# A merge stage whose branch products move from f32 matmuls to three-term split matmuls

## The chip, the cores and the metric

The kernel runs on one core of a Trainium2 chip. The metric is the device time of one execution in microseconds (us), the median of several runs. Engine names follow the profile: PE (TensorE, matmul), PEld (its weight load), DVE (VectorE), ACT (ScalarE), POOL (GpSimd), SP (SyncE, which here only sends DMAs).

## The reference

The program is two blocks in a row on a sequence of 1024 tokens of width 1024. The first has two layers, each with two recurrent branches; the second is attention, pooling and a mixture of experts. The change touches only the end of each layer of the first block, here called the merge:

```python
for l in range(DEPTH):                       # DEPTH = 2
    ...
    y_hg = o_hg.astype(x.dtype) @ w_branch_hg[l]       # (1024 x 512) @ (512 x 1024)
    ...
    y_rw = y_rw.astype(x.dtype) @ w_branch_rw[l]       # (1024 x 512) @ (512 x 1024)
    g_hg, g_rw = jnp.split(p_gate, N_BRANCH, axis=-1)
    merged = jax.nn.sigmoid(g_hg) * y_hg + jax.nn.sigmoid(g_rw) * y_rw
    out = merged @ w_out[l]                            # (1024 x 1024) @ (1024 x 1024)
    x = layer_norm(DN_ALPHA * x + (1.0 + gate_raw[:, None]) * out, ln_g[l], ln_b[l])
```

## The kernel before

The program is a chain of stages with a barrier of all engines behind each. `merge(k, l)` runs twice, once for each layer. Everything is held transposed: features on the 128 partitions in 8 tiles (`KT`), tokens along the free axis. The tokens are worked in two halves of 512 (`HALF`, `hf` = 0 and 1). Within a half there are two phases:

- Branch phase, 8 tiles (`branches(m)` on PE, m = 8 hf + j). For output tile j, PE makes the two branch products in f32, four matmuls each, from the raw weights `wb` (two buffers) and the branch outputs that the stages before left in `k.mix` (`k.yhg` and `k.yrw` are its halves). ACT takes the sigmoid of the loaded gates `sg` (`gates`). DVE (`merged`) multiplies both products by their gates (L2170), adds them (L2172), and splits the sum into a rounded high part (L2176, a CAST to float32r) and the rest, the low part (L2178). The two parts of all 8 tiles are `mS`.
- Product phase, 8 tiles (`product(q)` on PE). The weight slab `w` of output tile j is split the same way: ACT rounds it (`high`, L2123), POOL subtracts (L2109). PE then sums three products for each of 8 slices, in the order of `TERMS`: high x high, high x low, low x high, so 24 matmuls in one tile. ACT scales the result (`residual`), DVE adds it to the residual stream `xT` (`add`).

The layer norm over features follows: sums over the partitions by f32 matmuls with ones (`mean`, `variance`), `centre`, `squares`, `deviation` (rstd) and `normalise`. For the first half these are placed by hand in the branch phase of the second half; for the second half they stand at the end of the stage.

The order on each engine is the order of the code. Between the engines there are only semaphores that count finished operations: `hi_ready` and `lo_ready` for the parts of a slab, `slab_done` for a finished product tile, `ys_ready` for a finished branch product (two to a tile), `m_ready` and `mul_done` for DVE's multiplications and add, `low_ready` for the low part of `mS`. Each ring has two buffers: `w` and its parts `wS`, `wb`, `sg`, and the banks of `ps`. The loops of a stage are unrolled.

Of the kernel before, what the change touches and what calls it, by code (L numbers as in the profile page):

```python
# [2050 lines left out]
def merge(k, l):  # L2051
# [4 lines left out]
    with Stage(k, f"mix{l}") as s:  # L2056
        mS = s.sb("mS", [P, 2, KT, HALF], F32R)
        gate, lnp = s.sb("gate", [P, KT]), s.sb("lnp", [P, 2, KT])
        w, wS = s.sb("w", [P, 2, KT, P]), s.sb("wS", [P, 2, 2, KT, P], F32R)
        wb = s.sb("wb", [P, 2, KT, P])  # L2060
# [3 lines left out]
        ld_w, ld_wb, ld_sg = ([s.sem(f"{n}{b}") for b in range(2)] for n in ("ld_w", "ld_wb", "ld_sg"))  # L2064
# [10 lines left out]
        @block.sync
        def _(sp):
            def branch(m):
# [1 line left out]
                wait(sp, ys_ready, 2 * (m - 1))
                sp.dma_start(wb[:, b, 0:4], I["w_branch_hg"][l, j]).then_inc(ld_wb[b], 16)  # L2080
                sp.dma_start(wb[:, b, 4:8], I["w_branch_rw"][l, j]).then_inc(ld_wb[b], 16)
# [7 lines left out]
            sp.dma_start(lnp[:], I["ln_par"][l]).then_inc(ld_p, 16)
            branch(0)  # L2090
            branch(1)
            for hf in range(2):
                for j in range(2 if hf == 0 else 4, NJ):
                    branch(hf * NJ + j)
                    if j == 4 or j == 5:
                        slab(hf * NJ + j - 4)
                for j in range(2, NJ):
                    slab(hf * NJ + j)
                    if hf == 0 and j >= 6:
                        branch(NJ + j - 6)  # L2100
                if hf == 0:
                    branch(NJ + 2)
                    branch(NJ + 3)
# [35 lines left out]

# [1357 lines left out]
```

## Time and profile before

| | |
|---|---|
| median of 3 runs | 4628.94 us (4622.33 to 4638.01) |
| the profiled execution | 4627.36 us |
| its span, first to last instruction | 4625.1 us |
| PE busy | 4062.8 us, 88% of the span |
| DVE, ACT, POOL busy | 1684.2, 1205.4, 719.3 us |
| mean granted PE clock | 0.928 of full speed |
| first merge, first DMA issue to the next stage's first | 1125.76 to 1374.20 us |

The profile counts an engine as busy while one of its instructions runs. Matmuls overlap in PE's pipeline, so the duration of one record is longer than the distance between two; the price of a matmul is read from distances. An f32 matmul leaves two records in the trace, a float32r matmul one. Times in a timeline are microseconds from the start of the span.

### The profile page before, as it was taken

How to read it: one execution, taken by the hardware profiler on the slowest of the kernel's cores; microseconds unless marked ns; L12 is line 12 of the kernel's file. 1: busy time of each engine (PE TensorE's matmuls, PEld its weight loads, DVE VectorE, ACT ScalarE, POOL GpSimd, SP SyncE). 2: the span in 40 equal slices, each digit the busy share in tenths (PEclk: the TensorE clock that was granted, in tenths of full speed). 3: DMA queues.
4: the chain of work that ended last, by engine and by line, in shares of the span. 5: the costliest groups of instructions: out<-in, count | busy, mean ns of one | idle time of the engine just before them, and what ended most of it. 6: DMA issues, size and time to landing. Idle time of an engine off the chain costs nothing. (4 is left out here: it accounts for less than half of the span.)

```text
span 4625.1 us, 74505 instructions
## 1 busy us (share of the span) xinstructions
PE 4062.8 (88%) x29460; PEld 2648.0 (57%) x29460; DVE 1684.2 (36%) x2437; ACT 1205.4 (26%) x1715; POOL 719.3 (16%) x554
## 2 busy tenths in 40 slices
PE   6999888887979998888879978887889999999963
PEld 3888667665547887666655544535544444444423
DVE  3355554553341004545533426522511111111128
ACT  1111354442221112454422334412111111111114
POOL 2222122120122221131111100000010000000014
PEclk8999998898999999998889989997999999999985
DMA  6765333113313423331123217001089999999967
GB/s 218 216 220 177 124 112 123 53 44 117 127 68 134 141 100 121 107 126 63 39 88 123 86 44 295 35 32 58 19 303 356 351 360 359 356 357 355 355 249 263
DMA packets 289081, 795.16 MB, mean 172 GB/s; under 512 B 29377, under 2 KB 121026, under 8 KB 252994
## 3 DMA queue, kind: packets, MB, share of 16 engines
q1 hardware_dynamic: 240738, 616.41, 38.3%
q10 hardware_dynamic: 25632, 93.33, 5.0%
q0 software_dynamic: 22464, 81.80, 4.9%
q8 instruction: 195, 3.19, 0.3%
q14 instruction: 52, 0.43, 0.0%
HBM read 622.64 MB, written 160.43 MB: 169 GB/s over the span
## 5 line engine op out<-in xcount | busy, mean ns | idle before, releaser
L463 PE MATMUL ps<-s_proj_hS,s_proj_wS 128*128 128x512 f32 x3216 | 768.7, 402 | 62.5 <-POOL s_proj_wS L353 62.5
L463 PEld LDWEIGHTS ps<-s_proj_hS,s_proj_wS 128*128 128x128 f32 x3216 | 615.0, 192 | 212.3 <-ACT s_proj_wS L413 63.4
L518 PE MATMUL ps<-gate_h,gate_w 128*128 128x512 f32 x1536 | 417.9, 424 | 33.8 <-PEq L146 19.3
L518 PEld LDWEIGHTS ps<-gate_h,gate_w 128*128 128x128 f32 x1536 | 296.2, 198 | 136.9 <-issue 52.1
L3181 PE MATMUL ps<-s_exp_gu,keep_hT 128*128 128x512 f32 x736 | 340.9, 606 | 19.8 <-DMA s_exp_gu<-in_w_gu_dram 18.0
L3165 PE MATMUL ps<-s_exp_wd,s_exp_aT 128*128 128x512 f32 x736 | 331.2, 593 | 1.9 <-ACT s_exp_aT L3091 1.9
L3186 PE MATMUL ps<-s_exp_gu,keep_hT 128*128 128x512 f32 x736 | 330.8, 592 | 0.0
L505 POOL TENSOR_TENSOR gate_w<-gate_raw,gate_w 128x512 fp32r<-128x512 f32 x128 | 186.4, 1459 | 824.3 <-ACT gate_w L499 823.5
L3131 DVE TENSOR_TENSOR s_exp_sg<-s_exp_sg,ps 128x256 f32<-128x256 f32 x92 | 38.7, 421 | 666.6 <-ACT s_exp_sg L3112 666.6
L353 POOL TENSOR_TENSOR s_proj_wS<-s_proj_w,s_proj_wS 128x1024 fp32r<-128x1024 f32 x67 | 174.0, 2599 | 565.4 <-ACT s_proj_wS L413 565.4
L381 DVE COPY s_proj_o<-ps 128x512 f32<-128x512 f32 x66 | 45.5, 690 | 570.3 <-PE ps L463 570.3
L2225 PE MATMUL ps<-keep_mix,s_mix_wb 128*128 128x512 f32 x512 | 224.6, 600 | 27.1 <-DMA s_mix_wb<-in_w_branch_rw_dram 27.1
L3186 PEld LDWEIGHTS ps<-s_exp_gu,keep_hT 128*128 128x128 f32 x736 | 139.9, 190 | 176.3 <-issue 169.9
L3181 PEld LDWEIGHTS ps<-s_exp_gu,keep_hT 128*128 128x128 f32 x736 | 134.1, 192 | 166.9 <-issue 157.9
L3065 POOL COPY s_exp_idx<-keep_idx 128x1 int32 (+1 forms) x92 | 16.8, 183 | 1286.2 <-PE ps L3148 878.9
L3123 DVE COPY keep_hT<-ps 128x512 f32<-128x512 f32 x184 | 126.5, 687 | 246.3 <-PE ps L3165 223.7
L3165 PEld LDWEIGHTS ps<-s_exp_wd,s_exp_aT 128*128 128x128 f32 x736 | 132.7, 190 | 134.6 <-issue 132.5
L413 ACT ACTIVATE s_proj_wS<-s_proj_w 128x1024 fp32r<-128x1024 f32 x67 | 70.8, 1059 | 496.4 <-DVE s_proj_o L381 228.9
L2237 PE MATMUL ps<-s_mix_mS,s_mix_wS 128*128 128x512 f32 x768 | 193.7, 409 | 2.1 <-DVE s_mix_mS L2178 2.1
L3091 ACT ACTIVATE keep_hT<-ps 128x512 f32<-128x512 f32 x184 | 109.9, 597 | 327.1 <-PE ps L3165 273.6
L2225 PEld LDWEIGHTS ps<-keep_mix,s_mix_wb 128*128 128x128 f32 x512 | 98.4, 193 | 152.9 <-issue 123.6
L2237 PEld LDWEIGHTS ps<-s_mix_mS,s_mix_wS 128*128 128x128 f32 x768 | 144.5, 188 | 47.2 <-issue 11.5
(451 smaller groups left out, 5854.1 us busy)
## 6 DMA issues: line engine op xcount, KB each, us to landing
s_exp_gu<-in_w_gu_dram SPq DMA_DIRECT2D x184, 1024.0 KB, 10.8
s_exp_wd<-in_w_down_dram SPq DMA_DIRECT2D x92, 1024.0 KB, 9.1
yrow<-keep_hT ACTq DMA_DIRECT2D x92, 512.0 KB, 9.5
keep_mix<-in_w_ada_dram SPq DMA_DIRECT2D x80, 512.0 KB, 6.0
s_proj_w<-in_w_in_dram SPq DMA_DIRECT2D x66, 512.0 KB, 4.6
proj<-s_proj_o ACTq DMA_DIRECT2D x66, 512.0 KB, 2.7
gate_raw<-in_w_in_dram SPq DMA_DIRECT2D x128, 256.0 KB, 3.1
yrow<-keep_xT SPq DMA_DIRECT2D x4, 8192.0 KB, 49.1
```

The lines of the kernel that those rows point to most:

```text
L353: pool.tensor_tensor(wS[:, b, 1], w[:, b], wS[:, b, 0], ALU.subtract).then_inc(lo_ready, 1)
L413: act.activation(wS[:, b, 0], w[:, b], ACT.Copy).then_inc(hi_ready, 1)
L463: mm = pe.matmul(k.ps[:, 6 + half if last else 2 * b + half, :], wS[:, b, x, t, :], hS[:, y, t, half * HALF:(half + 1) * HALF], start=(t = ...
L505: pool.tensor_tensor(self.w[:, n % RING, 1], self.raw[:, n % 2], self.w[:, n % RING, 0], ALU.subtract).then_inc(self.split_low, 1)
L518: mm = pe.matmul(self.k.ps[:, self.banks[g // 2], :], weight[:, w, t - t0, :], self.k.hG[:, h, t, :], start=(t == 0 and w + h == 0), stop= ...
L2225: mm = pe.matmul(k.ps[:, 2 * b + g, :], wb[:, b, 4 * g + x, :], y[:, x, cut(hf)], start=(x == 0), stop=(x == 3))
L2237: mm = pe.matmul(k.ps[:, 4 + b, :], wS[:, b, u, x, :], mS[:, v, x, :], start=(x == 0 and u + v == 0), stop=(x == KT - 1 and u == 1))
L3091: return act.activation(o, i, ACT.Copy)
L3123: return dve.tensor_copy(o, i)
L3165: mm = pe.matmul(k.ps[:, 4 + half, :], aT[:, f, :], wd[:, u, f, half * HALF:(half + 1) * HALF], start=(f == 0), stop=(f == 1))
L3181: mm = pe.matmul(k.ps[:, 2 if u == 0 else 6, :], xT[:, u, t, :], gu[:, u, t, :], start=(t == 0), stop=False)
L3186: mm = pe.matmul(k.ps[:, 2 if u == 0 else 6, :], xT[:, u, t, :], gu[:, u, t, :], start=False, stop=(t == KT - 1))
```

## The change

The branch products now work as the output products do, on split parts. `wb` is gone. One ring of slabs, numbered z = `at(hf, j, out)`, carries the branch weights (`out` = 0) and `w_out` (`out` = 1) in the order in which PE takes them, each loaded by two DMAs; ACT and POOL split all 32 of a merge. The branch outputs are split as well, into `yS`: `inputs(0, x)` at the start of the stage, `inputs(1, x)` one slice behind each product tile of half 0. PE's branch tile is 24 matmuls in place of 8. On DVE, `normalise(0)` moves from the branch phase of half 1 into its product phase, one tile behind each `add`.

```diff
+        yS = s.sb("yS", [P, 2, KT, HALF], F32R)
-        wb = s.sb("wb", [P, 2, KT, P])
...
+        def at(hf, j, out):
+            return 2 * NJ * hf + NJ * out + j
+        def used(eng, z):
+            hf, out, j = z // (2 * NJ), z // NJ % 2, z % NJ
+            if out:
+                eng.wait_ge(slab_done, NJ * hf + j + 1)
+            else:
+                eng.wait_ge(ys_ready, 2 * (NJ * hf + j + 1))
...
+            def slab(z):
+                hf, out, j, b = z // (2 * NJ), z // NJ % 2, z % NJ, z % 2
+                wait(sp, lo_ready, z - 1)
+                for x in range(2):
+                    src = I["w_out"][l, j, :, 4 * x:4 * x + 4, :] if out else I[("w_branch_hg", "w_branch_rw")[x]][l, j]
+                    sp.dma_start(w[:, b, 4 * x:4 * x + 4], src).then_inc(ld_w[b], 16)
...
+            for z in range(4 * NJ):
+                pool.wait_ge(hi_ready, z + 1)
+                pool.tensor_tensor(wS[:, z % 2, 1], w[:, z % 2], wS[:, z % 2, 0], ALU.subtract).then_inc(lo_ready, 1)
...
+            def high(z):
+                if z < 4 * NJ:
+                    act.wait_ge(ld_w[z % 2], 32 * (z // 2 + 1))
+                    if z >= 2:
+                        used(act, z - 2)
+                    act.activation(wS[:, z % 2, 0], w[:, z % 2], ACT.Copy).then_inc(hi_ready, 1)
+            def inputs(hf, x):
+                if hf:
+                    act.wait_ge(ys_ready, 2 * NJ)
+                act.activation(yS[:, 0, x], k.mix[:, x, cut(hf)], ACT.Copy).then_inc(yh_ready, 1)
...
+            high(0)
+            for x in range(KT):
+                inputs(0, x)
+            high(1)
             act.wait_ge(gate_ready, 1)
             for hf in range(2):
                 for j in range(NJ):
                     gates(hf * NJ + j)
+                    high(at(hf, j + 2, 0))
...
                 for j in range(NJ):
                     residual(hf * NJ + j)
-                    if j + 2 < NJ:
-                        high(hf * NJ + j + 2)
+                    high(at(hf, j + 2, 1))
+                    if hf == 0:
+                        inputs(1, j)
...
+            def inputs(hf, x):
+                dve.wait_ge(yh_ready, hf * KT + x + 1)
+                dve.tensor_tensor(yS[:, 1, x], k.mix[:, x, cut(hf)], yS[:, 0, x], ALU.subtract).then_inc(yl_ready, 1)
...
-                    if hf and j == 5:
-                        normalise(0)
                 for j in range(NJ):
                     add(hf * NJ + j)
+                    if hf == 0:
+                        inputs(1, j)
+                    else:
+                        normalise(0, range(j, j + 1))
...
             def branches(m):
-                hf, b = m // NJ, m % 2
+                hf, j, b = m // NJ, m % NJ, m % 2
+                z = at(hf, j, 0)
+                pe.wait_ge(hi_ready, z + 1)
+                pe.wait_ge(lo_ready, z + 1)
                 wait(pe, m_ready, 2 * (m - 1))
-                pe.wait_ge(ld_wb[b], 32 * (m // 2 + 1))
-                for g, y in enumerate((k.yhg, k.yrw)):
-                    for x in range(4):
-                        mm = pe.matmul(k.ps[:, 2 * b + g, :], wb[:, b, 4 * g + x, :], y[:, x, cut(hf)], start=(x == 0), stop=(x == 3))
-                    mm.then_inc(ys_ready, 1)
+                for x in range(KT):
+                    if j == 0:
+                        pe.wait_ge(yl_ready, hf * KT + x + 1)
+                    for u, v in TERMS:
+                        mm = pe.matmul(k.ps[:, 2 * b + x // 4, :], wS[:, z % 2, u, x, :], yS[:, v, x, :],
+                                       start=(x % 4 == 0 and u + v == 0), stop=(x % 4 == 3 and u == 1))
+                    if x == 3:
+                        mm.then_inc(ys_ready, 1)
+                mm.then_inc(ys_ready, 1)
```

ACT at the start of the merge. Before, its queue was:

```order
 L2118 ACT_TABLE_LOAD
 L2118 ACTIVATE s_mix_sg<-s_mix_sg 128x1024 x6
 L2123 ACTIVATE s_mix_wS<-s_mix_w 128x1024
 L2118 ACTIVATE s_mix_sg<-s_mix_sg 128x1024
 L2123 ACTIVATE s_mix_wS<-s_mix_w 128x1024
```

In the changed kernel (L2140 is `high`, L2145 `inputs`, L2133 `gates`) it is:

```order
 L2140 ACTIVATE s_mix_wS<-s_mix_w 128x1024
 L2145 ACTIVATE s_mix_yS<-keep_mix 128x512 x8
 L2140 ACTIVATE s_mix_wS<-s_mix_w 128x1024
 L2133 ACT_TABLE_LOAD
 L2133 ACTIVATE s_mix_sg<-s_mix_sg 128x1024
 L2140 ACTIVATE s_mix_wS<-s_mix_w 128x1024
```

The first gates now stand behind two high parts and eight copies, and every later gate tile has a high part behind it.

PE around the turn from half 0 to half 1. This is one piece of the queue before (L2225 `branches`, L2237 `product`, L2243 `mean`, L2250 `variance`):

```order
 L2237 MATMUL ps<-s_mix_mS,s_mix_wS 128x512 x24
 L2243 MATMUL ps<-keep_xT,keep_ones 128x512
 L2225 MATMUL ps<-keep_mix,s_mix_wb 128x512 x8
 L2243 MATMUL ps<-keep_xT,keep_ones 128x512 x2
 L2225 MATMUL ps<-keep_mix,s_mix_wb 128x512 x24
 L2250 MATMUL ps<-s_mix_sq,keep_ones 128x512 x8
```

and the same piece of the changed kernel (L2261 `branches`, L2276 `product`, L2282 `mean`, L2289 `variance`):

```order
 L2276 MATMUL ps<-s_mix_mS,s_mix_wS 128x512 x24
 L2282 MATMUL ps<-keep_xT,keep_ones 128x512
 L2261 MATMUL ps<-s_mix_yS,s_mix_wS 128x512 x24
 L2282 MATMUL ps<-keep_xT,keep_ones 128x512 x2
 L2261 MATMUL ps<-s_mix_yS,s_mix_wS 128x512 x72
 L2289 MATMUL ps<-s_mix_sq,keep_ones 128x512 x8
```

Nothing changes places on PE; each branch tile has 24 matmuls in place of 8.

DVE at the end of half 1's branch phase. Before, `normalise(0)` (L2198, L2201) stood between branch tiles:

```order
 L2178 TENSOR_TENSOR s_mix_mS<-s_mix_tmp,s_mix_mS 128x512
 L2198 TENSOR_TENSOR keep_xT<-keep_xT,s_mix_rstd 128x512 x8
 L2201 TENSOR_SCALAR keep_xT<-keep_xT,s_mix_lnp 128x512 x8
 L2170 TENSOR_TENSOR s_mix_sg<-s_mix_sg,ps 128x512 x2
 L2172 TENSOR_TENSOR s_mix_tmp<-s_mix_sg 128x512
```

In the changed kernel it stands between the additions (L2211 `add`, L2226 and L2229 `normalise`), tile by tile, behind the last branch tile (L2202):

```order
 L2202 TENSOR_TENSOR s_mix_mS<-s_mix_tmp,s_mix_mS 128x512
 L2211 SCALAR_TENSOR_TENSOR keep_xT<-keep_xT,s_mix_t 128x512
 L2226 TENSOR_TENSOR keep_xT<-keep_xT,s_mix_rstd 128x512
 L2229 TENSOR_SCALAR keep_xT<-keep_xT,s_mix_lnp 128x512
 L2211 SCALAR_TENSOR_TENSOR keep_xT<-keep_xT,s_mix_t 128x512
```

Sixteen DVE operations have moved from one place to eight.

## Rows read from the trace of the kernel before

**Rows 1.** The profile's page: span, and busy time of each engine.

```profile
span 4625.1 us, 74505 instructions
PE 4062.8 (88%) x29460; PEld 2648.0 (57%) x29460; DVE 1684.2 (36%) x2437; ACT 1205.4 (26%) x1715; POOL 719.3 (16%) x554
```

**Rows 2.** PE's timeline, both merges: start, duration, engine, line, operation, count, idle before.

```profile
1129.53 56.91 PE L2225 MATMUL ps<-keep_mix,s_mix_wb 128*128 128x512 f32 x128 [13.27 <-DMA s_mix_wb<-in_w_branch_rw_dram]
1185.88 17.42 PE L2237 MATMUL ps<-s_mix_mS,s_mix_wS 128*128 128x512 f32 x72
...
1244.91 20.76 PE L2225 MATMUL ps<-keep_mix,s_mix_wb 128*128 128x512 f32 x48
1265.51 7.03 PE L2250 MATMUL ps<-s_mix_sq,keep_ones 128*128 128x512 f32 x16
...
1305.98 12.21 PE L2237 MATMUL ps<-s_mix_mS,s_mix_wS 128*128 128x512 f32 x51 [1.06 <-DVE s_mix_mS L2178]
...
2603.03 12.21 PE L2237 MATMUL ps<-s_mix_mS,s_mix_wS 128*128 128x512 f32 x51 [1.01 <-DVE s_mix_mS L2178]
```

**Rows 3.** The timeline at the start of the first merge, SyncE's DMA queue.

```profile
1125.76 0.33 SPq L2089 DMA_DIRECT2D s_mix_lnp<-in_ln_par_dram  x1
```

**Rows 4.** ACT's timeline, the first two product tiles.

```profile
1192.09 0.69 ACT L2128 ACTIVATE s_mix_t<-ps,s_mix_gate 128x512 f32<-128x512 f32 x1 [12.16 <-PE ps L2237]
...
1197.72 0.69 ACT L2128 ACTIVATE s_mix_t<-ps,s_mix_gate 128x512 f32<-128x512 f32 x1 [3.99 <-PE ps L2237]
```

**Rows 5.** Groups by line and form, first merge: count, busy, mean ns, idle before.

```profile
L2237 PE MATMUL ps<-s_mix_mS,s_mix_wS 128*128 128x512 f32 x384 | 96.8, 409 | 1.1 <-DVE s_mix_mS L2178 1.1
...
L2109 POOL TENSOR_TENSOR s_mix_wS<-s_mix_w,s_mix_wS 128x1024 fp32r<-128x1024 f32 x16 | 38.6, 2413 | 178.8 <-ACT s_mix_wS L2123 178.8
...
L2123 ACT ACTIVATE s_mix_wS<-s_mix_w 128x1024 fp32r<-128x1024 f32 x16 | 16.8, 1048 | 0.0
L2118 ACT ACTIVATE s_mix_sg<-s_mix_sg 128x1024 f32<-128x1024 f32 x16 | 16.8, 1054 | 63.8 <-DMA s_mix_sg<-gates 63.8
```

**Rows 6.** Windows: length, busy time (and instructions) of each engine, granted clock, DMA.

```profile
1130.00:1134.00 4.00, 4.00 (x7) 1.50 (x7) 0.00 (x0) 1.72 (x2) 0.00 (x0) 0.62 0.85 305
...
1185.00:1235.00 50.00, 50.00 (x204) 38.22 (x203) 7.35 (x11) 10.51 (x13) 14.40 (x6) 1.00 0.25 85
```

**Rows 7.** Timelines of DVE and of POOL, branch tiles 5 and 6, half 0.

```profile
1173.47 0.69 DVE L2172 TENSOR_TENSOR s_mix_tmp<-s_mix_sg 128x512 f32<-128x512 f32 x1
1174.19 2.46 DVE L2176 CAST s_mix_mS<-s_mix_tmp 128x512 fp32r<-128x512 f32 x1
...
1181.06 0.43 DVE L2176 CAST s_mix_mS<-s_mix_tmp 128x512 fp32r<-128x512 f32 x1
...
1167.16 2.35 POOL L2109 TENSOR_TENSOR s_mix_wS<-s_mix_w,s_mix_wS 128x1024 fp32r<-128x1024 f32 x1 [42.84 <-ACT s_mix_wS L2123]
1173.60 2.77 POOL L2109 TENSOR_TENSOR s_mix_wS<-s_mix_w,s_mix_wS 128x1024 fp32r<-128x1024 f32 x1 [4.09 <-ACT s_mix_wS L2123]
```

**Rows 8.** Timelines of DVE and of ACT, half 1: the layer norm of half 0.

```profile
1254.49 4.87 DVE L2189 SCALAR_TENSOR_TENSOR keep_xT<-ps,keep_xT 128x512 f32<-128x512 f32 x8
...
1287.03 2.77 DVE L2172 TENSOR_TENSOR s_mix_tmp<-s_mix_sg 128x512 f32<-128x512 f32 x1
...
1290.90 4.90 DVE L2198 TENSOR_TENSOR keep_xT<-keep_xT,s_mix_rstd 128x512 f32<-128x512 f32 x8
1295.84 3.74 DVE L2201 TENSOR_SCALAR keep_xT<-keep_xT,s_mix_lnp 128x512 f32<-128x512 f32 x8
...
1255.21 4.81 ACT L2133 ACTIVATE s_mix_sq<-keep_xT 128x512 f32<-128x512 f32 x8 [5.33 <-DVE keep_xT L2189]
```

**Rows 9.** DMA issues, first merge: count, KB each, median us to landing.

```profile
s_mix_sg<-gates SPq DMA_DIRECT2D x16, 512.0 KB, 4.5
...
s_mix_wb<-in_w_branch_rw_dram SPq DMA_DIRECT2D x16, 256.0 KB, 2.9
```

**Rows 10.** The tile `wS`, POOL, both merges: shortest, median and longest in ns.

```profile
L2109 POOL TENSOR_TENSOR s_mix_wS<-s_mix_w,s_mix_wS x32: 2345/2401/2787, 1167.2 to 2636.4; 128x1024 fp32r<-128x1024 f32 x32
```

More of the change, by code:

```diff
@@ L2063, in merge @@
         sq, rstd = s.sb("sq", [P, KT, HALF]), s.sb("rstd", [P, HALF])
-        ld_w, ld_wb, ld_sg = ([s.sem(f"{n}{b}") for b in range(2)] for n in ("ld_w", "ld_wb", "ld_sg"))
+        ld_w, ld_sg = ([s.sem(f"{n}{b}") for b in range(2)] for n in ("ld_w", "ld_sg"))
+        yh_ready, yl_ready = s.sem("yh_ready"), s.sem("yl_ready")
         ld_p = s.sem("ld_p")
@@ L2076, in _, with gates @@
         def _(sp):
[L2077 removed]
+            def slab(z):
[4 more added lines that the diff above has]
+                    sp.dma_start(w[:, b, 4 * x:4 * x + 4], src).then_inc(ld_w[b], 16)
+            def gates(m):
                 hf, j, b = m // NJ, m % NJ, m % 2
[L2079 to L2081 removed]
@@ L2082, in branch @@
                 wait(sp, mul_done, m - 1)
                 sp.dma_start(sg[:, b], k.scratch["gates"][hf, j]).then_inc(ld_sg[b], 16)
-            def slab(q):
-                wait(sp, lo_ready, q - 1)
-                sp.dma_start(w[:, q % 2], I["w_out"][l, q % NJ]).then_inc(ld_w[q % 2], 16)
             sp.dma_start(lnp[:], I["ln_par"][l]).then_inc(ld_p, 16)
-            branch(0)
-            branch(1)
+            slab(0)
+            slab(1)
+            gates(0)
+            gates(1)
             for hf in range(2):
[L2093 to L2098, printed above, removed]
+                for j in range(NJ):
+                    if hf == 0 and j >= 2:
+                        gates(j)
+                    if hf and j >= 2:
+                        gates(NJ + j)
+                    slab(at(hf, j + 2, 0))
+                for j in range(NJ):
@@ L2099, in _ @@
                     if hf == 0 and j >= 6:
[L2100 to L2103, printed above, removed]
+                        gates(NJ + j - 6)
+                    if at(hf, j + 2, 1) < 4 * NJ:
+                        slab(at(hf, j + 2, 1))
         @block.gpsimd
         def _(pool):
-            for q in range(NM):
-                pool.wait_ge(hi_ready, q + 1)
-                pool.tensor_tensor(wS[:, q % 2, 1], w[:, q % 2], wS[:, q % 2, 0], ALU.subtract).then_inc(lo_ready, 1)
+            for z in range(4 * NJ):
+                pool.wait_ge(hi_ready, z + 1)
+                pool.tensor_tensor(wS[:, z % 2, 1], w[:, z % 2], wS[:, z % 2, 0], ALU.subtract).then_inc(lo_ready, 1)
@@ L2190, in centre, with normalise @@
                        .then_inc(xc_ready, 1)
-            def normalise(hf):
+            def normalise(hf, tiles):
                 dve.wait_ge(ld_p, 16)
@@ L2196, in normalise @@
                 dve.wait_ge(rstd_ready, hf + 1)
-                for j in range(KT):
+                for j in tiles:
                     mine.mark(dve.tensor_tensor(k.xT[:, j, cut(hf)], k.xT[:, j, cut(hf)], rstd[:], ALU.mult))
                 mine.settle()
-                for j in range(KT):
+                for j in tiles:
                     mine.mark(dve.tensor_scalar(k.xT[:, j, cut(hf)], k.xT[:, j, cut(hf)], lnp[:, 0, j:j + 1], lnp[:, 1, j:j + 1],
@@ L2209, in _ @@
                         centre(0)
-                    if hf and j == 5:
-                        normalise(0)
                 for j in range(NJ):
                     add(hf * NJ + j)
+                    if hf == 0:
+                        inputs(1, j)
+                    else:
+                        normalise(0, range(j, j + 1))
             centre(1)
-            normalise(1)
+            normalise(1, range(KT))
         @block.tensor
```

18 lines of the change are left out of this document (6 added, 12 removed).

## The prediction

> **What bounds the kernel now.** I read the page first: PE is busy 4062.8 us of a span of 4625.1 [rows 1], so the first question is whether PE also sets the time inside the two merges, which are all that the change touches. PE's timeline answers it. In the first merge PE starts at 1129.53 and then runs without a break to 1305.98, where it has waited 1.06 us for the last piece of `mS`; the second merge shows the same one wait, of 1.01 us [rows 2]. Work taken from PE between those points therefore shortens the kernel, until something else ends last. What PE waits for ahead of 1129.53 is the first branch weights: the stage's first DMA is issued at 1125.76 [rows 3].
>
> Two prices come out of these rows. A branch tile is 8 f32 matmuls: three of them run from 1244.91 to 1265.51, 20.60 us, so **6.87 us a tile** (0.859 a matmul) [rows 2]. A product tile is 24 matmuls on split operands; ScalarE takes the results of the first two products at 1192.09 and 1197.72, so **5.62 us a tile**, 0.234 a matmul [rows 4]. The time of one record (409 ns for L2237 [rows 5]) is no price, as records overlap. The windows show the clock at 1.00, that is 2.4 GHz, in the products, and 0.62 in the first 4 us of the stage, mostly 1.2 GHz, after PE had stood idle for 13.27 us [rows 2, 6].
>
> **The change part by part.**
>
> *Branch products.* The new branch tile has the same 24 matmuls of 128x512 on operands of the same kind as a product tile, so I take 5.62 us: 6.87 - 5.62 = 1.25 us off each of 32 tiles (16 in each merge), 40.0 us if nothing else moved.
>
> The same step by another price: the Trainium skill (VectorE: DVE Perf Modes, the section on the TRN2 errata) gives 6 + 512 cycles at 2.4 GHz for such a matmul, 216 ns. By that the tile would be an estimated 5.18 us and the step 54 us. The trace has 234 ns for the very same matmul, and goes first.
>
> *The start of each merge.* Before, PE needs only the raw weights. Now it needs the weight slab's high part from ACT (1.05 us, L2123), its low part from POOL (2.41, L2109) [rows 5], and the first slice of `yS` (ACT copy, DVE subtraction 0.69 like the other 128x512 DVE operations [rows 7]). DVE cannot do that subtraction beside POOL's: where POOL subtracts from 1173.60 (2.77 long), DVE's CAST that began at 1174.19 takes 2.46, not the 0.43 of 1181.06, and POOL's own is longer than the 2.35 of 1167.16, as DVE's add was still running [rows 7]. So one waits for the other's whole instruction. From the landing at 1129.53: 1.05, 2.41, 0.69 and three handoffs of 0.1 make 1133.9 for PE's first matmul, 4.4 us later than before. Then seven more subtractions, about 0.64 each back to back (0.61 to 0.69 by the eight of L2198, 4.90 us [rows 8]). Slab 1's high part stands behind ACT's eight copies of 0.60 (4.81 for eight, L2133 [rows 8]): 1130.6 + 4.8 + 1.05 = 1136.5. POOL then takes its turn among DVE's subtractions and pushes the last of them by 2.4, to about 1140.8; three matmuls later, at 1141.5, tile 0 ends. If POOL has to wait for all eight instead, slab 1 is ready at 1140.8 and the end is 1140.9, so this hardly matters. The slow clock at the start is inside: before it cost 56.35 - 8 x 6.87 = 1.4 us [rows 2], here PE waits for DVE anyway. Seven tiles of 5.62 more end at 1180.8; before, the products began at 1185.88. Half 0 gains **5.1 us**, not 10.0.
>
> *A tile in the middle.* Counted from the end E of branch tile j: ACT's high part of slab j+2 lasts to E+1.1, POOL's low part to E+3.6. DVE multiplies and adds to E+1.5, its CAST waits for POOL to about E+3.9, and it is done at E+5.1, below 5.62. PE needs slab j+2 only at E+5.62, and the multiplications of tile j by then. The gate load is sent after the add at E+1.5 and lands 4.5 us later [rows 9], with the sigmoid (1.05, L2118 [rows 5]) done at E+7.2, due at E+11.2. So each chain fits, DVE's by only 0.5 us. SyncE's queue: two slab halves and a gate load a tile, the same 1 MB as before, in a shorter tile; each half (like `wb`, 2.9 us [rows 9]) is sent after POOL's low part of two tiles back and has over 3 us to spare.
>
> *Half 1.* Eight tiles give 10.0 us. `centre(0)` holds DVE 4.87 us and ACT's squares 4.81 [rows 8], but PE's eight matmuls of `variance` (6.87 us) come just behind and let them catch up. `deviation` now stands behind a high part; its table loads and the next sigmoid's delay slab 7 to about the moment at which it is due. `normalise(0)`, 4.90 + 3.74 us on DVE [rows 8], leaves the branch phase, and with it goes most of the reason for the wait of 1.06 us. In the products it adds about 1.3 us a tile to a DVE that does one add in 5.6 us; the last tile's share ends about when the mean does, so 0 to 0.2.
>
> *New small waits.* The last `mS` slice of half 0 is done near E+5.1 where PE wants it at E+4.9 (seven of its eight steps of 0.70): 0.2 to 0.4. The last `yS` slice for half 1: 0 to 0.2. The last `mS` slice of half 1, with its sigmoid late: 0.3 to 0.9. I take 0.9 in all a merge (0.5 to 1.5).
>
> *The sum.* A merge: 5.1 + 10.0 + 1.06 - 0.9 = 15.3; two merges 30.6. The profiled execution took 4627.36 us, so 4596.8; the median of the runs is 1.6 us above it, which gives **4598 us**.
>
> What only bounds: how often DVE and POOL collide. With no collision at all a merge gains about 17 (34 in all). With each POOL subtraction as long as the longest of 32, 2.79 [rows 10], the low part ends at E+4.0 to 4.4, DVE finishes at 5.5 to 5.9 and a tile is at most 0.3 longer: 10 us less, a gain of 21. I stay near the middle, as their median is 2.40.
>
> **Rivals.**
>
> *The clock stays low.* At the start PE's matmuls come in threes at DVE's pace with a hole of 2.4 us in them, not in a full stream. If the granted clock then stays at 1.2 GHz to the end of tile 1, that tile takes 11.2 instead of 5.6: 5.6 us more a merge, a gain of 19, 4609 us. For it: 0.62 in the first 4 us even in a full stream [rows 6]. Against: half of the matmuls' time is still there.
>
> *DVE becomes the bound, and the kernel slower.* If POOL's subtraction blocked both the add (2.77 [rows 8]) and the CAST (2.46) in each tile, DVE would take 0.69 x 2 + 2.77 + 2.46 + 0.69 = 7.3 us a tile. That is 0.4 above 6.87: 14 us lost on 32 tiles, and 9 at the two starts, 4650 us. The point from which it decides is a tile of about 6.6 us. Against: a tile has one POOL instruction, and after it both DVE operations are free. The Trainium skill (SBUF — State Buffer, Who interferes with whom) calls this an exclusive lock held for one instruction, which speaks against a double block; no row here shows one.
>
> *The matmul is faster than in the products.* An f32 matmul takes four times 0.215 us. Were each of the three records 0.215 and not 0.234, a tile would be 5.16 and the gain about 15 us larger, 4583. DVE at 5.1 would just follow. The skill's 216 ns says the same; the product rows speak against it.
>
> *The change does too little to see*, 4615 to 4643: the starts and the late sigmoid of half 1 cost double of what I have, and tiles run at 6.1. No single row speaks for it.
>
> **How the numbers follow.** The forecast (4590 to 4606) gets 0.70, the low clock with some longer tiles (4606 to 4615) 0.13, the faster matmul or no collisions (below 4590) 0.06, too little to see 0.07, slower 0.04. The range 4588 to 4612 holds a little over 8 in 10. A measurement of this kernel tells 0.3%, about 14 us, from no change; faster by more has 0.88, within it 0.08, slower 0.04.
>
> **What the new profile would show.** Branch tiles 5.6 us apart by the first multiplication of each tile; the clock at 1.00 from the second tile on. First matmul of the merge 4 to 5 us later after the stage's first DMA, and a hole in tile 0 while POOL works. CASTs of about 2.5 us in most branch tiles, with PE not waiting. PE waits below 1 us at each change between branches and products. `normalise(0)` between the adds of half 1. Wrong would be: tiles over 6 us with PE released by the slab's low part or by DVE, or a clock below 1.00 behind tile 1.

## The result and the profile after

| | before | changed |
|---|---|---|
| median of 4 runs each, same chip | 4629.66 us (4622.33 to 4638.01) | 4587.77 us (4581.16 to 4592.45) |
| profiled execution, its time | 4627.36 | 4590.06 |
| first merge, first DMA issue to the next stage's | 248.44 | 230.54 |
| second merge | 248.40 | 230.86 |

The ratio is 0.991, with an interval of 0.9892 to 0.9929: faster, by 41.9 us of medians where 30.6 were forecast. 4587.77 lies 0.23 us under the low end of the range. The two traces show 17.90 + 17.54 = 35.4 us in the merges; the rest comes back below. Nine of the kernels below ran once; between runs of one kernel the time scatters by some 10 to 20 us, so these are read by their traces.

The page, first lines, answering to [rows 1], and the rows of the new branch products and of POOL's subtractions in its list of groups:

```profile
span 4588.3 us, 75257 instructions
PE 4012.9 (87%) x29716; PEld 2689.6 (59%) x29716; DVE 1813.7 (40%) x2469; ACT 1251.6 (27%) x1779; POOL 797.8 (17%) x586
...
L2261 PE MATMUL ps<-s_mix_yS,s_mix_wS 128*128 128x512 f32 x768 | 184.1, 401 | 35.1 <-DVE s_mix_yS L2206 35.0
...
L2124 POOL TENSOR_TENSOR s_mix_wS<-s_mix_w,s_mix_wS 128x1024 fp32r<-128x1024 f32 x64 | 159.4, 2490 | 240.2 <-ACT s_mix_wS L2140 240.2
```

PE lost 50 us of work and the kernel 37 of span. POOL's subtractions doubled from 32 to 64. PE's timeline, first merge and one row of the second, answering to [rows 2]:

```profile
1131.53 46.25 PE L2261 MATMUL ps<-s_mix_yS,s_mix_wS 128*128 128x512 f32 x192 [17.54 <-DVE s_mix_yS L2206]
1177.62 17.14 PE L2276 MATMUL ps<-s_mix_mS,s_mix_wS 128*128 128x512 f32 x72
...
1234.60 16.94 PE L2261 MATMUL ps<-s_mix_yS,s_mix_wS 128*128 128x512 f32 x72
1251.38 7.03 PE L2289 MATMUL ps<-s_mix_sq,keep_ones 128*128 128x512 f32 x16
1257.85 22.66 PE L2261 MATMUL ps<-s_mix_yS,s_mix_wS 128*128 128x512 f32 x96
1280.34 5.07 PE L2276 MATMUL ps<-s_mix_mS,s_mix_wS 128*128 128x512 f32 x21
1285.67 12.21 PE L2276 MATMUL ps<-s_mix_mS,s_mix_wS 128*128 128x512 f32 x51 [0.26 <-DVE s_mix_mS L2202]
...
2565.37 12.21 PE L2276 MATMUL ps<-s_mix_mS,s_mix_wS 128*128 128x512 f32 x51 [0.27 <-DVE s_mix_mS L2202]
```

The start of the merge (timelines of SyncE's queue, ACT, POOL and DVE), answering to [rows 3]:

```profile
1123.49 0.33 SPq L2102 DMA_DIRECT2D s_mix_lnp<-in_ln_par_dram  x1
1127.35 1.06 ACT L2140 ACTIVATE s_mix_wS<-s_mix_w 128x1024 fp32r<-128x1024 f32 x1 [10.36 <-DMA s_mix_w<-in_w_branch_rw_dram]
1128.48 2.35 POOL L2124 TENSOR_TENSOR s_mix_wS<-s_mix_w,s_mix_wS 128x1024 fp32r<-128x1024 f32 x1 [6.44 <-ACT s_mix_wS L2140]
1128.96 8.83 DVE L2206 TENSOR_TENSOR s_mix_yS<-keep_mix,s_mix_yS 128x512 fp32r<-128x512 f32 x8 [5.26 <-ACT s_mix_yS L2145]
1133.59 2.44 POOL L2124 TENSOR_TENSOR s_mix_wS<-s_mix_w,s_mix_wS 128x1024 fp32r<-128x1024 f32 x1 [2.75 <-ACT s_mix_wS L2140]
```

PE's first matmul stands 8.04 us behind the first DMA issue, where it stood 3.77 behind. DVE's eight slices take 8.83 us, not 4.9 to 5.2, since POOL's two subtractions (1128.48, 1133.59) lie among them.

DVE's timeline in a steady stretch of branch tiles, answering to [rows 7], and the tile view of `mS` on DVE (ns: shortest, median, longest):

```profile
1156.06 0.69 DVE L2194 TENSOR_TENSOR s_mix_sg<-s_mix_sg,ps 128x512 f32<-128x512 f32 x1 [0.16 <-PE ps L2261]
1156.78 0.69 DVE L2196 TENSOR_TENSOR s_mix_tmp<-s_mix_sg 128x512 f32<-128x512 f32 x1
1157.51 2.51 DVE L2200 CAST s_mix_mS<-s_mix_tmp 128x512 fp32r<-128x512 f32 x1
1160.05 0.69 DVE L2202 TENSOR_TENSOR s_mix_mS<-s_mix_tmp,s_mix_mS 128x512 fp32r<-128x512 f32 x1
1160.66 0.68 DVE L2194 TENSOR_TENSOR s_mix_sg<-s_mix_sg,ps 128x512 f32<-128x512 f32 x1
1161.50 0.69 DVE L2194 TENSOR_TENSOR s_mix_sg<-s_mix_sg,ps 128x512 f32<-128x512 f32 x1 [0.16 <-PE ps L2261]
```

```profile
L2200 DVE CAST s_mix_mS<-s_mix_tmp x32: 427/2506/2511, 1141.2 to 2562.1; 128x512 fp32r<-128x512 f32 x32
```

The same multiplication stands 5.44 us later (1156.06, 1161.50): that is a branch tile, and PE releases each one, 0.16 us after DVE came free. The multiplication of the next tile's first product (1160.66) belongs to the same 5.44 us, so DVE has only 0.16 us of them to spare. The CAST takes 2.5 us in 23 of 32 tiles (in 4 of 32 before), and no PE wait follows from it.

Windows over the start, answering to [rows 6] (busy time of PE, of its weight loads, then DVE, ACT, POOL; clock; DMA):

```profile
1130.00:1134.00 4.00, 2.47 (x6) 2.02 (x7) 4.00 (x6) 3.98 (x7) 1.25 (x2) 0.50 0.70 236
1134.00:1138.00 4.00, 4.00 (x14) 3.11 (x13) 4.00 (x4) 1.87 (x2) 2.04 (x1) 0.65 0.24 58
1138.00:1142.00 4.00, 4.00 (x19) 3.33 (x18) 2.58 (x4) 2.01 (x2) 1.05 (x1) 1.00 0.20 75
```

PE had been idle for 17.54 us and starts at 0.50, the 1.2 GHz level; from 1138 on, inside tile 0, it is at 1.00.

### The profile page after: what moved, and what is told of

Its sections match the earlier page's. It is cut to its first block and busy times, and to the rows that moved or that the text cites. A ratio compares the mean times of both kernels' runs of the same rounds, so it can differ in the third digit from the quotient of the medians.

```text
span 4588.3 us, 75257 instructions
## 1 busy us (share of the span) xinstructions
PE 4012.9 (87%) x29716; PEld 2689.6 (59%) x29716; DVE 1813.7 (40%) x2469; ACT 1251.6 (27%) x1779; POOL 797.8 (17%) x586
## 5 line engine op out<-in xcount | busy, mean ns | idle before, releaser
L518 PE MATMUL ps<-gate_h,gate_w 128*128 128x512 f32 x1536 | 415.1, 422 | 35.4 <-PEq L146 19.3
L2261 PE MATMUL ps<-s_mix_yS,s_mix_wS 128*128 128x512 f32 x768 | 184.1, 401 | 35.1 <-DVE s_mix_yS L2206 35.0
L2124 POOL TENSOR_TENSOR s_mix_wS<-s_mix_w,s_mix_wS 128x1024 fp32r<-128x1024 f32 x64 | 159.4, 2490 | 240.2 <-ACT s_mix_wS L2140 240.2
L2276 PE MATMUL ps<-s_mix_mS,s_mix_wS 128*128 128x512 f32 x768 | 192.3, 407 | 0.5 <-DVE s_mix_mS L2202 0.5
L2261 PEld LDWEIGHTS ps<-s_mix_yS,s_mix_wS 128*128 128x128 f32 x768 | 147.6, 193 | 72.1 <-issue 41.1
```

The source lines that it names most:

```text
L518: mm = pe.matmul(self.k.ps[:, self.banks[g // 2], :], weight[:, w, t - t0, :], self.k.hG[:, h, t, :], start=(t == 0 and w + h == 0), stop= ...
L2124: pool.tensor_tensor(wS[:, z % 2, 1], w[:, z % 2], wS[:, z % 2, 0], ALU.subtract).then_inc(lo_ready, 1)
L2261: mm = pe.matmul(k.ps[:, 2 * b + x // 4, :], wS[:, z % 2, u, x, :], yS[:, v, x, :], start=(x % 4 == 0 and u + v == 0), stop=(x % 4 == 3 an ...
L2276: mm = pe.matmul(k.ps[:, 4 + b, :], wS[:, z % 2, u, x, :], mS[:, v, x, :], start=(x == 0 and u + v == 0), stop=(x == KT - 1 and u == 1))
```

## The experiments

All merge times are first DMA issue to the next stage's first, from each profile. "Branch" and "product" are the distances of two matmuls in a tile, in ns, from the starts of PE's records: the median over stretches of 12 with no record missing, good to about 0.5. "Place" is the byte in a partition at which a tile starts, worked out from the order and sizes of the tiles. In the changed kernel `mS` starts at 88800 (32 past a multiple of 64), `yS` at 121664 and `wS` at 162624 (multiples of 64). The number in brackets is a remainder in bytes: the start of `wS` less the start of the moving tile (`yS` or `mS`), divided by 512. The steps inside the tiles (512 bytes between the slices of `wS`, 2048 between those of a moving tile) are multiples of 512, so it is the same for every matmul of a tile. An empty cell was not needed for the argument.

| kernel | time, us (runs) | merges, us | branch | product |
|---|---|---|---|---|
| changed | 4587.8 (4) | 230.5, 230.9 | 226.7 (0) | 234.2 (96) |
| swap_starts | 4592.8 (1) | 232.1, 232.2 | 233.3 (32) | 232.6 (128) |
| weights_off | 4591.7 (1) | 232.7, 232.5 | 233.3 (32) | 233.3 (160) |
| all_at_0 | 4594.5 (1) | 229.4, 230.2 | 226.7 (0) | 232.8 (128) |
| all_at_64 | 4591.3 (1) | 230.1, 230.1 | 226.7 (0) | 233.3 (128) |
| product_two_banks | 4612.2 (1) | 232.1, 232.2 | 226.7 (0) | 232.6 (128) |
| places_swapped | 4587.4 (1) | 229.1, 229.9 | 232.8 (128) | 226.7 (0) |
| product_reads_yS | 4583.6 (1) | 229.0, 229.4 | 226.7 (0) | half 0 232.6 (128), half 1 226.7 (0) |
| align_all | 4585.8 (1) | 230.1, 230.7 | 226.7 (0) | 232.9 (128) |
| norm_back | 4605.4 (4) | 243.2, 243.2 | | |
| norm_only | 4630.7 (10) | 247.5, 248.4 | | |
| pool_twice | 4611.9 (1) | 240.1, 239.3 | | |
| changed_again | 4587.0 (5) | 231.1, 230.8 | | |
| first_tile_f32 | 4593.6 (4) | 230.2, 228.9 | | |
| first_tile_own | 4580.4 (6) | 226.7, 226.6 | 226.7 (0) | 233.3 (128) |
| weights_between | 4582.5 (4) | 227.7, 226.5 | 226.7 (0) | 232.8 (128) |

**Why is a branch matmul faster than a product matmul?** Same instruction, same operand types, 24 a tile; but 5.44 against some 5.6 us. A first pair of kernels moves the places by 32 bytes:

```diff
+        padm = s.sb("padm", [P, 8])
         mS = s.sb("mS", [P, 2, KT, HALF], F32R)
...
         yS = s.sb("yS", [P, 2, KT, HALF], F32R)
+        padw = s.sb("padw", [P, 8])
         w, wS = ...
```

> The changed kernel with two pads of 32 bytes, so that mS starts at a multiple of 64 bytes and yS 32 bytes past one; wS stays at a multiple of 64. In the changed kernel it is the other way round, and a branch tile takes 5.44 us, a product tile 5.62. Theory 1 (the start address of the moving operand sets the distance of two matmuls): the branch tile goes to 5.62 (0.234 a matmul), the product tile to 5.44 (0.227). Theory 2 (the branch tile is faster because its 24 matmuls go to two PSUM banks in two chains of 12, not one of 24): nothing changes, 5.44 and 5.62.

The branch products got slow: DVE's multiplications of two branch tiles stand at 1153.31 and 1158.91, 5.60 us. The product did not get 227. So two pads of 32 bytes cost the branch its advantage, with the same code; by theory 1 that is the start off the multiple of 64, and something else holds the product back. The second kernel has one more pad, ahead of `yS`, so that `mS` and `yS` are right and `wS` is 32 past:

> The changed kernel with three pads: mS and yS both start at a multiple of 64 bytes, wS 32 bytes past one. Theory 1a (only the moving operand's start matters): both tiles take 5.44. Theory 1b (the weights' start matters too): both take 5.62. Theory 2 (PSUM chains): 5.44 and 5.62 as now.

Both were slow (233.3 each), with `yS` at its right start: the weights' start counts as well. With all three at multiples of 128 (pads ahead of `mS` and `yS` alone), and then all at odd multiples of 64:

> The changed kernel with pads so that mS, yS and wS all start at a multiple of 128 bytes. So far: branch matmuls 0.227 us apart where yS and wS both lie 64 bytes past a multiple of 128 (the changed kernel), 0.233 where either lies 32 bytes past a multiple of 64; product matmuls 0.2327 with mS and wS at a multiple of 128. Theory A (a multiple of 64 for both operands is what counts, and the product tile has another limit, one chain in one bank): branch 0.227, product 0.233. Theory B (both operands must lie 64 past a multiple of 128): branch 0.233 too, product 0.233.

> The changed kernel with pads so that mS, yS and wS all start 64 bytes past a multiple of 128. Theory A (the product tile has a limit of its own): branch 0.227, product 0.233. Theory B (the start addresses alone decide): branch and product both 0.227, a product tile 5.44 us, and a merge some 2.5 to 3 us shorter than 230.5.

Both came out alike: branch 226.7, product 232.8 and 233.3. A multiple of 64 is enough for the branch, and it is not enough for the product. What else differs is the accumulation (one chain of 24 into one bank, against two of 12) and the tile's place. The chain first:

```diff
-  mm = pe.matmul(k.ps[:, 4 + b, :], ..., start=(x == 0 and u + v == 0), stop=(x == KT - 1 and u == 1))
+  mm = pe.matmul(k.ps[:, b if x < 4 else 4 + b, :], ..., start=(x % 4 == 0 and u + v == 0), stop=(x % 4 == 3 and u == 1))
```

This kernel, product_two_banks, leaves the first half of each output sum out of the residual. The experts behind it then get other numbers, and perhaps other work, so only its merges are compared. One more wait (not shown) holds the first product of a half until DVE has read the branch banks.

> The changed kernel with all three operands at a multiple of 128 bytes, and each product tile written as two chains of 12 matmuls to two PSUM banks, as a branch tile is; the residual takes only the second, so half of each product sum is left out of the result. Theory (a chain of 24 in one bank is what keeps product matmuls at 0.233 with aligned operands): 0.227 apart in the products too, a merge some 2.5 to 3 us under all_at_0 (229.4 to 230.2). Rival (it is something else in the product tile, such as mS itself): 0.233 as in all_at_0.

Product 232.6 ns: the chain is not it. The merges, 232.1 and 232.2 us, are longer: in the first of them PE waits 0.98 and 1.36 us ahead of the first products of the two halves, where all_at_0 has no wait. Now the two tiles change places, all at multiples of 128:

```diff
-        mS = s.sb("mS", ...)
+        yS = s.sb("yS", ...)
         gate, lnp = ...
-        yS = s.sb("yS", ...)
+        mS = s.sb("mS", ...)
```

> As all_at_0 (all three operands at a multiple of 128 bytes), with yS and mS in each other's place in the partition: yS now lies below mS. So far with aligned operands: branch 0.227, product 0.233. Theory P (where the moving operand lies against the weights decides): the product tile gets 0.227 and the branch tile 0.233. Rival Q (something in the product phase itself, the data or what the other engines do): 0.227 and 0.233 as in all_at_0.

The advantage changed sides. DVE's multiplications of two branch tiles of places_swapped (5.60 apart):

```profile
1151.28 0.69 DVE L2196 TENSOR_TENSOR s_mix_sg<-s_mix_sg,ps 128x512 f32<-128x512 f32 x1 [0.31 <-PE ps L2263]
...
1156.88 0.69 DVE L2196 TENSOR_TENSOR s_mix_sg<-s_mix_sg,ps 128x512 f32<-128x512 f32 x1 [0.31 <-PE ps L2263]
```

and ACT's first two product results of the same kernel, 5.45 us apart where [rows 4] has 5.63:

```profile
1185.01 0.69 ACT L2152 ACTIVATE s_mix_t<-ps,s_mix_gate 128x512 f32<-128x512 f32 x1 [4.61 <-PE ps L2278]
...
1190.46 0.69 ACT L2152 ACTIVATE s_mix_t<-ps,s_mix_gate 128x512 f32<-128x512 f32 x1 [3.29 <-PE ps L2278]
```

To hold layout and code equal, half 1's products of all_at_0 read `yS` in place of `mS`; the output of that half is then not the layer's.

```diff
+ wS[:, z % 2, u, x, :], (yS if q >= NJ else mS)[:, v, x, :],
```

> As all_at_0, with the products of half 1 taken from yS in place of mS, so that the output of that half is not the layer's; half 0 is the control. Theory P (the place of mS decides): half 1's products 0.227 apart, half 0's 0.233. Rival Q (the product phase itself: its weights, its banks, what ACT and DVE do beside it): 0.233 in both halves. Under either, a merge gets at most 1.5 us shorter.

Half 0's products 232.6 ns, half 1's 226.7; merges 228.96 and 229.43. So it goes with where the moving operand lies, not with the phase. Is it its distance from the weights, or the place itself? The next kernel is first_tile_own (below) with `w` and `wS` between the two: `mS` 88832, `wS` 129920, `yS` 146304.

> As first_tile_own (all three at a multiple of 128 bytes), with the slabs w and wS placed between mS and yS in the partition, so that both moving operands lie next to the weights. Shown so far: with aligned starts the moving operand in the upper place, 33 to 66 KB nearer to wS, gets 0.227, the one in the lower place 0.233, whichever of the two it is. Theory N (nearness to the weights decides): 0.227 in both phases, a product tile 5.46, a merge 2 us under the 226.7 of first_tile_own. Rival A (the absolute place, low is slow): products stay at 0.233 and a merge at 226.7, branch 0.227. Rival S (the operand must lie below the weights and near them): branch 0.233, product 0.227.

Branch 226.7, product 232.8: `mS`, now next to the weights, stayed slow, and the nearness theory fell. 4582.45 us, ratio 0.9899 (0.9877 to 0.992). Last, the other stages with such matmuls (projections, gates), where one of the operands starts 32 past, were padded to multiples of 64 by 32 bytes ahead of them:

> The changed kernel with 32-byte pads that bring the operands of the projections (L463), the gate slabs (L518), the merges and the ones matrix to a multiple of 64 bytes; the recurrent stage of the second branch goes to 32 past one by it. Now projection matmuls are 0.2334 apart, gate matmuls 0.2341. Theory from the branch tiles (both operands at a multiple of 64 are enough): 0.227 for both, 21 and 11 us off. Rival from the product tiles, which stayed at 0.2327 with aligned operands (a chain of 24 in one bank has its own limit): 0.2327 for both, 2 us each.

By the measure of the table, the projections' matmul stayed at 233.3 ns and the gates' went from 234.2 to 232.8, not to 227. One run, 4585.76: no gain to be told.

These runs leave two readings. The first needs two conditions for a fast matmul: both operands start at a multiple of 64 bytes, and the moving one starts at 121664 or above (88896 and below were slow). The second needs one, the remainder in the table: it is 0 in every fast case and in no slow one, and the distance goes with it from tile to tile. At 32 it is 233.3 ns, for the branches of swap_starts and weights_off and for the projections alike; at 96 it is 234.2, for the products of the changed kernel and for the gates; at 128 it is 232.6 to 233.3; the projections of align_all have 64, 233.3, and its gates 128, 232.8. No kernel separates the two: none has a moving tile in the low place with a remainder of 0, which 384 bytes between `mS` and `yS` in all_at_0 would give. What is shown is that the layout sets the distance; which property of it does is open.

**What is moving `normalise(0)` worth?** In the changed kernel it is put back behind branch tile 5 of half 1:

```diff
                     if hf and j == 1:
                         centre(0)
+                    if hf and j == 5:
+                        normalise(0, range(KT))
...
                     if hf == 0:
                         inputs(1, j)
-                    else:
-                        normalise(0, range(j, j + 1))
```

> The changed kernel with the normalisation of half 0 put back behind branch tile 5 of half 1. It measures what the move was worth. My theory (little, as in the prediction): DVE is held 4.90 + 3.74 us there, while a branch tile now takes 5.44 and DVE has 0.5 us to spare in each, so it comes late to the last tiles: PE waits 3 to 5 us for mS at the first product tile of half 1 in place of 0.26, and a merge takes 233.5 to 235.5 us in place of 230.5; 6 to 10 us in all. Rival (the move was not needed): a merge takes at most 231.5 us, the wait stays near the 1.06 of before.

4605.41 us, ratio to before 0.993 to 0.9963, some 18 us above the changed kernel by the medians, and 12.6 and 12.3 us more in the merges, 25 together: far over the expectation. PE's timeline of norm_back:

```profile
1278.11 4.37 PE L2276 MATMUL ps<-s_mix_mS,s_mix_wS 128*128 128x512 f32 x18
1290.51 1.65 PE L2276 MATMUL ps<-s_mix_mS,s_mix_wS 128*128 128x512 f32 x3 [8.02 <-DVE s_mix_mS L2202]
1293.62 14.49 PE L2276 MATMUL ps<-s_mix_mS,s_mix_wS 128*128 128x512 f32 x51 [1.46 <-DVE s_mix_mS L2202]
```

and DVE's, where the normalisation stands:

```profile
1274.12 9.32 DVE L2226 TENSOR_TENSOR keep_xT<-keep_xT,s_mix_rstd 128x512 f32<-128x512 f32 x8
1283.48 3.74 DVE L2229 TENSOR_SCALAR keep_xT<-keep_xT,s_mix_lnp 128x512 f32<-128x512 f32 x8
```

The same eight multiplications that took 4.90 us before [rows 8] take 9.32, since POOL now subtracts twice among them (1273.77 and 1279.51), and with the 3.74 behind them hold the last two `mS` slices up: PE waits 8.02 and 1.46. That is 9.2 us more than the 0.26 of the changed kernel. The other 3 us are the clock. Windows of norm_back (PE, its weight loads, DVE, ACT, POOL; clock; DMA):

```profile
1294.00:1296.00 2.00, 2.00 (x6) 1.52 (x6) 0.00 (x0) 0.70 (x2) 0.00 (x0) 0.50 0.00 0
1300.00:1302.00 2.00, 2.00 (x10) 1.63 (x9) 0.00 (x0) 0.00 (x0) 0.00 (x0) 1.00 0.74 252
```

Behind the wait of 8.02 us the granted clock stands at 0.50, the 1.2 GHz level, and it is back at 1.00 by 1300: some 15 matmuls are 427 ns or more apart and not 234, some 3 us. The expectation counted neither this nor the collision. The same move alone, in the kernel before:

> The kernel before with the move of the normalisation of half 0 alone: tile by tile behind the additions of half 1, branch products in f32 as before. By the prediction the move takes away the wait of 1.06 us and little else: a merge goes from 248.4 to 247.4 (247.2 to 247.8), the whole from 4629 to 4626, not to be told from no change. Rival, since putting it back into the changed kernel cost 12.6 us a merge: the move is worth several us in the kernel before too, a merge of 244 or less.

4630.67 us, ratio 0.9997 to 1.002: nothing, though the wait of 1.06 us is gone; the first merge took 247.5 us, as expected, the second 248.4, as before. So the move is worth at most 1 us a merge by itself, and 12.3 to 12.6 behind the other edits.

**How near is the branch phase to DVE's and POOL's limit?** POOL's subtraction is done twice for each branch slab from the third on:

```diff
+                if z // NJ % 2 == 0 and z >= 2:
+                    pool.tensor_tensor(wS[:, z % 2, 1], w[:, z % 2], wS[:, z % 2, 0], ALU.subtract).then_inc(extra, 1)
+                    pool.wait_ge(extra, ...)
                 pool.tensor_tensor(wS[:, z % 2, 1], w[:, z % 2], wS[:, z % 2, 0], ALU.subtract).then_inc(lo_ready, 1)
```

> The changed kernel with POOL's subtraction done twice for every branch slab from slab 2 on (the same result written twice), about 2.45 us more for each. It asks how much room the chain from slab to tile has. My theory: ACT's high part ends 1.1 us behind the end of a tile, two subtractions 6.0 to 6.2, above 5.44, so the next but one tile starts 0.6 to 0.8 late: a branch tile goes to 5.8 to 6.0 on average, and a merge to 236 to 240 us. Rival (DVE is the engine with no room; blocked twice by POOL it takes 7.3 us a tile or more): branch tiles of 7 us or more, a merge of 250 us or more.

9.5 and 8.4 us more a merge (240.1 and 239.3), at the upper end of what was expected, and the tiles a little above it. PE's timeline of pool_twice, two tiles to a row:

```profile
1145.15 11.37 PE L2265 MATMUL ps<-s_mix_yS,s_mix_wS 128*128 128x512 f32 x48 [0.90 <-issue]
1157.66 11.19 PE L2265 MATMUL ps<-s_mix_yS,s_mix_wS 128*128 128x512 f32 x48 [1.14 <-issue]
1169.91 11.20 PE L2265 MATMUL ps<-s_mix_yS,s_mix_wS 128*128 128x512 f32 x48 [1.06 <-issue]
```

12.25 to 12.5 us a pair, so 6.1 to 6.3 a tile: a POOL step of 2.4 us more costs 0.7 to 0.8 a tile, the rest was slack. What PE waits for is the slab's low part: POOL's second subtraction ends at 1167.11 + 2.70 = 1169.81, and PE starts at 1169.91. DVE, blocked by both subtractions, has no idle time in these tiles either. This comes near the double block that the rival on DVE named, and it stays under 6.87.

**Can the start be had back?** The cost of splitting the first slab is avoided if tile 0 of a merge stays in f32, on the raw slab and `k.mix`. That is first_tile_f32:

```diff
+                if m == 0:
+                    pe.wait_ge(ld_w[0], 32)
+                    for x in range(KT):
+                        mm = pe.matmul(k.ps[:, x // 4, :], w[:, 0, x, :], k.mix[:, x, cut(0)], ...)
```

> The changed kernel, with the first branch tile of each merge in f32 from the raw slab and the unsplit branch outputs, so that PE starts when the first weights land; the parts of slab 1 and of the first half of yS are made meanwhile, and slab 0 is never split. Theory (PE is late at the start only because the first tile waits for parts): first matmul 3.8 us after the stage's first DMA in place of 8.05; tile 0 ends at 12.5 in place of 16.2; tile 1 starts at 12.5 to 13.5, the rest as now: a merge of 227 to 228 in place of 230.5, 5 to 7 us in all. Rival (DVE's subtractions and POOL's collide as before and end at the same time, so tile 1 starts at 16 anyway): a merge of 230 or more.

Half of it: the first matmul stands at +3.77 us again, as before, and tile 1 starts at +13.4 (1139.07), as the theory had it and not the rival. But the third slab is loaded into the raw buffer only when tile 0 has been read, and PE waits for it, as the timelines of PE, ACT and POOL show:

```profile
1129.44 10.19 PE L2258 MATMUL ps<-keep_mix,s_mix_w 128*128 128x512 f32 x16 [13.26 <-DMA s_mix_w<-in_w_branch_rw_dram]
...
1146.65 32.92 PE L2269 MATMUL ps<-s_mix_yS,s_mix_wS 128*128 128x512 f32 x144 [1.53 <-issue]
...
1143.02 1.06 ACT L2142 ACTIVATE s_mix_wS<-s_mix_w 128x1024 fp32r<-128x1024 f32 x1 [3.70 <-DMA s_mix_w<-in_w_branch_rw_dram]
...
1144.16 2.39 POOL L2126 TENSOR_TENSOR s_mix_wS<-s_mix_w,s_mix_wS 128x1024 fp32r<-128x1024 f32 x1 [8.93 <-ACT s_mix_wS L2142]
```

POOL ends at 1146.55, and PE starts 0.1 us later. 4593.61 us, ratio 0.9897 to 0.994; the merges, 230.15 and 228.91, are over the 227 to 228 of the theory. The changed kernel was measured again:

> The changed kernel itself once more, in five rounds. In its trace the two merges are 17.9 and 17.5 us shorter than before, 35.4 together, while the medians of the first comparison lie 41.9 us apart. Theory (the merges are the whole of the gain, and the other 6 us are scatter between executions): 4590 to 4595 beside a kernel before of 4625 to 4630, a difference of 33 to 38 us. Rival (the change helps elsewhere too): 40 us or more once more.

4586.97 us (4584.13 to 4588.77), ratio 0.9912 (0.9898 to 0.9926); its merges are 35.0 us shorter than before, its median 39.35, between the two expectations.

first_tile_own adds a buffer `w0` for the first raw slab, sends the third slab at once, and has `mS`, `yS` and `wS` at multiples of 128:

```diff
+        w0, ld_0 = s.sb("w0", [P, KT, P]), s.sem("ld_0")
...
             gates(0)
+            slab(2)
             gates(1)
```

> As first_tile_f32, with a buffer of its own for the first raw slab, so that slab 2 is loaded at once and no longer waits for the end of tile 0, and with mS, yS and wS at a multiple of 128 bytes. In first_tile_f32 PE waited 1.6 us ahead of tile 2 for slab 2. Theory: that wait goes, tile 1 starts at 12.1 to 13.4 as there, branch matmuls 0.227 and product matmuls 0.233 apart, a merge of 226.5 to 228.5 in place of 230.5 to 230.9, the whole 5 to 8 us under the changed kernel of the same call. Rival (the longer time at the low clock at the start eats it): a merge of 230 again.

PE's timeline of first_tile_own, whose first DMA issue stands at 1118.36: the wait is gone.

```profile
1122.17 8.97 PE L2262 MATMUL ps<-keep_mix,s_mix_w 128*128 128x512 f32 x16 [13.31 <-DMA s_mix_w<-in_w_branch_rw_dram]
1130.58 38.67 PE L2273 MATMUL ps<-s_mix_yS,s_mix_wS 128*128 128x512 f32 x168
```

Merges 226.71 and 226.62 us, 3.8 and 4.2 under the changed kernel's. 4580.37 us (4570.87 to 4589.51, 6 runs), ratio 0.9905 (0.989 to 0.992). It has the lowest median, 6.6 us under changed_again; since the runs overlap, the 8 us in the merges are the firmer number.

## Why the prediction was right, and where it was not

*How far off.* The median came out 10.2 us under the 4598 of the forecast. 4.8 of them lie in the merges (35.4 us where 30.6 were forecast); by these alone it would have been 4593, inside the range. The other 5.4 lie outside the merges, see the last paragraph.

*What bounds.* Right. From its first matmul on, PE ran through but for small waits, and what was taken from it shortened the kernel.

*The start.* 4.3 us later to the first matmul where 4.4 were worked out, by the chain named. Tile 0 ended 16.2 us after the first DMA issue (DVE's first multiplication of the tile's second half stands at 1139.74) where the sum had 15.7. Half 0's products start 54.13 us after the issue, 60.12 before: 6.0 gained, 5.1 forecast. The clock rival was wrong, by the windows above.

*The failed step* is this one: "The new branch tile has the same 24 matmuls of 128x512 on operands of the same kind as a product tile, so I take 5.62 us". It measured 5.44, 0.2267 a matmul. The seven tiles behind tile 0 and the eight of half 1 make 15 x 0.18 = 2.7 us a merge. A merge then gains 15.3 + 2.7, less the 0.5 of tile 0 and with 0.3 less of small waits (below): 17.8 us, against 17.90 and 17.54 in the traces. The mechanism of the forecast stood; this term was mis-sized, by 5.4 us in both merges. What took its place: a tile's price depends on where its operands lie in the partition, and the price had come from a tile, `mS`, that lies otherwise. With the same code, two pads of 32 bytes put the branch tile back to 5.60 us (swap_starts). Whether it is the start and place of the moving tile or the remainder between the two starts is open. Of the rival "the matmul is faster than in the products" the direction was right and the size was not: 0.2267, not 0.215. The 216 ns that the Trainium skill states (VectorE: DVE Perf Modes, the TRN2 errata) was reached by no split matmul of any run here; nearest came 226.7.

*A tile in the middle.* Right in the outcome, with some luck: DVE's chain was reckoned at E+5.1 and fits even 5.44. E is 1155.9 above; DVE ends at 1160.05 + 0.69 = 1160.74, E+4.8. But "DVE's by only 0.5 us" left out the multiplication of the next tile's first product, which follows (1160.66, 0.68 us). With it the reckoned chain would have come to E+5.8, above the tile; the measured one leaves 0.16 us. pool_twice shows what POOL's slack is worth. The whole-instruction block between DVE and POOL held in the rows read here (CAST 0.43 alone, 2.5 beside POOL), as the Trainium skill says of that lock (SBUF — State Buffer, Who interferes with whom), and by the timelines it cost PE nothing in the steady tiles.

*Half 1.* Slab 7 was said to come "about the moment at which it is due", at no cost. ACT's copy of it ran from 1271.16, behind `deviation`'s table loads, and POOL's low part from 1272.29 (2.40 us). Four tiles of 5.44 from 1257.85, with the 0.4 by which the first distance of a row is longer at every change from f32 to split matmuls (here 631 ns), would end at 1280.01, and the products began at 1280.34: some 0.3 us of PE waiting that the timeline shows only as a longer row. It stands ahead of the last of the four tiles, where two distances are 415 and 306 ns. With the 0.26 ahead of half 1's products the small waits came to 0.6, where 0.9 were taken.

*`normalise(0)`.* Its move cost nothing, as forecast. But "with it goes most of the reason for the wait of 1.06 us" weighed it at one us; by norm_only and norm_back it is worth that at most in the old kernel and 12.3 to 12.6 us a merge in the new one. The forecast was not hurt, since it counted the kernel with both; a reader who had left the move out by that sentence would have lost 25 us in the merges.

*What is left over.* The medians differ by 41.9 us (and 39.35 in the second measurement), the merges by 35. Outside the two merges, the profiled time was 4130.5 us before and 4128.7 after, and 4117.5 to 4139.9 over the runs with the same code there. The 4 to 7 us beyond the merges are within that scatter; that it is scatter alone was argued, not shown.

## What to carry to other kernels

When a tile's work on one engine is cut, ask of every job that sits beside it whether it still fits: the same move was worth nothing in the old kernel and 25 us of merge time in the new one. Count with a long wait of PE what the clock takes behind it: here 3 us behind 8. A price taken from the same instruction on another tile holds to some 3% only, as the layout changed it here; note the starts of both operands with it, and the difference between them. Where an engine waits at a stage's start for preparation, let the first tile run unprepared, with a buffer of its own so that its late release holds no load up.

## What the hardware showed that was not expected

- The distance of two split 128x512 matmuls hangs on where the operands lie in the partition: 226.7 ns in some layouts, 232.6 to 234.2 in others. Two readings fit every run: both starts at a multiple of 64 bytes with the moving tile at 121664 or above (146304 was the highest), or a difference of the two starts that is a multiple of 512 bytes (16384 and 40960 were measured; remainders of 32, 64, 96, 128 and 160 were slow). Which of them it is, and why, stays open.
- Eight multiplications on DVE that take 4.90 us alone took 9.32 beside POOL's subtractions.
- After PE had waited 8.02 us in the middle of a stage, the granted clock was 0.50 and came back to 1.00 only by 1300, some 10 us after PE had gone on; some 15 matmuls took 427 ns or more each in place of 234 (norm_back).
